# One inference step with 32 experts: expert weights loaded as pairs of chunks, and four buffers for the h2 rows

## What is computed

```python
h = x + mix
ff = _moe(_rmsnorm(h, norm2_g), router_w, router_b, w1, b1, w2, b2)
# in _moe, for each block of rows of one expert e:
a = xe @ w1[e] + b1[e]                      # w1[e] is 1024 x 2048
glu = jnp.minimum(a[:, 0::2], SWIGLU_LIMIT)
lin = jnp.clip(a[:, 1::2], -SWIGLU_LIMIT, SWIGLU_LIMIT)
act = glu * jax.nn.sigmoid(SWIGLU_ALPHA * glu) * (lin + 1.0)
yb = act @ w2[e] + b2[e]                    # w2[e] is 1024 x 1024
# y = sum over the 4 experts of a row of gate * yb; then h + y, and a last norm
```

## Time and profile before

| | |
|---|---|
| median of 3 runs | 1410.18 us (1409.35 to 1410.38) |
| the profiled execution's own time | 1410.55 us |
| its span, first to last instruction | 1408.6 us |
| mean granted clock of TensorE | 0.977 |
| PE busy | 1314.7 us, 93% |
| DVE, ACT, POOL busy | 336.8, 236.8, 313.1 us |
| moved by DMA | 476.19 MB, 338 GB/s over the span |

### The profile page before, as it was taken

How to read it: one execution, slowest core, us unless ns; L and a number is a source line. 1 busy time by engine, 2 the same in 40 slices (tenths; PEclk the granted TensorE clock), 3 DMA queues, 4 the chain that set the end, 5 groups by cost and what they waited for, 6 DMA issues and landing times.

```text
span 1408.6 us, 36025 instructions
## 1 busy us (share of the span) xinstructions
PE 1314.7 (93%) x15410; PEld 664.1 (47%) x15411; DVE 336.8 (24%) x570; ACT 236.8 (17%) x554; POOL 313.1 (22%) x321
## 2 busy tenths in 40 slices
PE   5999869987989999999999999999999999999993
PEld 5999547985333333333333333333333333434332
DVE  4322674246111121111111121111111111211111
ACT  5433674132000000010000000010000000000012
POOL 1200000102632222223322222223222222222212
PEclk9999799997999999999999999999999999999996
DMA  8523404775999999999999999999999999999996
GB/s 243 169 81 107 146 1 152 272 285 192 351 408 398 407 406 407 407 407 406 402 402 402 407 406 406 407 407 406 403 403 402 403 407 406 406 406 406 406 404 180
DMA packets 104039, 476.19 MB, mean 338 GB/s; under 512 B 14158, under 2 KB 39370, under 8 KB 54737
## 3 DMA queue, kind: packets, MB, share of 16 engines
q1 hardware_dynamic: 81769, 443.39, 78.5%
q0 software_dynamic: 22224, 32.16, 9.5%
HBM read 457.02 MB, written 22.34 MB: 340 GB/s over the span
## 4 chain that ended last, share of the span: by engine, by line
PE 65%; DMA 20%; SPq 6%; DVE 4%; issue 2%; ACT 2%; POOL 1%; POOLq 0%; DVEq 0%; ACTq 0%
PE ps L1794 31%; PE ps L1817 18%; DMA freed<-w 14%; PE ps L1512 10%; SPq L486 5%; DMA h_rows<-raw 1%; DMA arena<-h_rows,idx_t 1%; PE ps L1800 1%; PE ps L1638 1%; POOL slot_table L653 1%; PE ps L1688 1%; SPq L468 1%; DMA raw<-w_in 1%; DVE arena L1173 1%; DMA cst<-c_misc 0%
## 5 line engine op out<-in xcount | busy, mean ns | idle before, releaser
L1794 PE MATMUL ps<-freed,arena 128*32 128x512 f32 x2976 | 332.3, 595 | 13.2 <-DMA freed<-w 6.7
L1794 PE MATMUL ps<-raw,arena 128*32 128x512 f32 x2976 | 327.4, 593 | 2.6 <-DMA raw<-w 2.5
L1817 PE MATMUL ps<-freed,act_t 128*32 128x256 f32 x5952 | 326.7, 379 | 0.0
L1817 PEld LDWEIGHTS ps<-freed,act_t 128*32 128x32 f32 x5952 | 188.0, 110 | 133.6 <-issue 0.7
L645 POOL DMA_INDIRECT sum_rows<-arena,idx_s x87 | 137.7, 1582 | 487.9 <-issue 487.9
L1794 PEld LDWEIGHTS ps<-raw,arena 128*32 128x32 f32 x2976 | 92.3, 110 | 232.1 <-issue 211.1
L1794 PEld LDWEIGHTS ps<-freed,arena 128*32 128x32 f32 x2976 | 92.5, 110 | 231.2 <-issue 205.3
L1386 DVE TENSOR_SCALAR arena<-ps 128x512 f32<-128x512 f32 x64 | 32.7, 553 | 622.0 <-PE ps L1800 622.0
L983 ACT ACTIVATE arena<-ps 128x256 f32<-128x256 f32 x64 | 31.4, 491 | 672.3 <-PE ps L1800 663.6
L1512 PE MATMUL ps<-hi,t_hi 128*128 128x256 f32 x400 | 115.8, 290 | 3.1 <-ACT raw L807 1.7
L1512 PE MATMUL ps<-lo,t_hi 128*128 128x256 f32 x400 | 114.0, 285 | 0.0
(11 more groups left out here) (258 smaller groups left out, 881.4 us busy)
## 6 DMA issues: line engine op xcount, KB each, us to landing
freed<-w SPq DMA_DIRECT2D x256, 1024.0 KB, 24.0
raw<-w SPq DMA_DIRECT2D x128, 1024.0 KB, 22.8
raw<-w_in SPq DMA_DIRECT2D x8, 1024.0 KB, 6.6
raw<-cache_k SPq DMA_DIRECT2D x32, 256.0 KB, 4.6
raw<-cache_v SPq DMA_DIRECT2D x32, 256.0 KB, 5.1
raw<-w_out SPq DMA_DIRECT2D x4, 1024.0 KB, 4.9
raw<-x_prompt SPq DMA_DIRECT2D x4, 512.0 KB, 4.0
arena<-x_prompt POOLq DMA_DIRECT2D x4, 512.0 KB, 5.8
```

Source lines behind the costliest of these rows:

```text
L1794: last = pe.matmul(ps[TR * b:TR * b + TR, i, :], x_of[:, at:at + TR], w[:, 512 * b:512 * b + 512], start=j == 0, stop=False, tile_position ...
L1817: last = pe.matmul(ps[TR * b:TR * b + TR, 3 + i, 0:QD], act_of[:, at:at + TR], w[:, col:col + QD], start=g == 0 and half == 0, stop=g == W ...
```

## The change

Weights of experts are loaded two chunks at a time: one DMA of 2 MB, 16 KB contiguous per partition in memory and on the chip. Twelve single slots become six pair buffers (`pair_at`), each with one semaphore; PE waits at every even chunk. A pair buffer is free when both its chunks were multiplied. The semaphores of the projection weights are their own now (`s_pro`), and `split_hi` and `split_lo` name raw's slot directly. `h2` takes raw's third and fourth slots and has four buffers: only the fifth tile waits, for the first tile's transposes and its store (`s_h2a`), and POOL issues each store as soon as its rows are there. The last of the first six pairs waits for all stores.

```diff
+        def pair_at(q):
+            if q == 0:
+                return raw[:, 0:2, :]
+            if q == RAW // 2 - 1:
+                return raw[:, 2:4, :]
+            at = (0, 4, 2, 6)[q - 1]
+            return freed[:, at:at + 2, :]
+
         def raw_at(s):
-            if s < 3:
-                return raw[:, s, :]
-            if s < RAW - 1:
-                return freed[:, RING * ((s - 3) % 2) + (s - 3) // 2, :]
-            return raw[:, 3, :]
+            return pair_at(s // 2)[:, s % 2, :]
...
-        h2 = raw[:, 3, :].rearrange("p (a n) -> p a n", a=2)
+        h2 = raw[:, 2:4, :].rearrange("p s (a n) -> p (s a) n", a=2)
...
             def load_expert(ck, j, e, k, second_half):
 
+                q = ck.raw_slot(j) // 2
                 if second_half:
-                    src = a["w2"][0][bass.ds(e, 1)].rearrange("a (p k) n -> (a p) k n", k=KT)[:, 2 * k:2 * k + 2, :]
-                    dst = raw_at(ck.raw_slot(j)).rearrange("p (k n) -> p k n", k=2)
+                    src = a["w2"][0][bass.ds(e, 1)].rearrange("a (p k) n -> (a p) k n", k=KT)[:, 2 * k:2 * k + 4, :]
+                    dst = pair_at(q).rearrange("p s (k n) -> p (s k) n", k=2)
                 else:
-                    src = a["w1"][0][bass.ds(e, 1)].rearrange("a (p k) n -> (a p) k n", k=KT)[:, k, :]
-                    dst = raw_at(ck.raw_slot(j))
-                return sp.dma_start(dst, src).then_inc(s_raw[ck.raw_slot(j)], 16)
+                    src = a["w1"][0][bass.ds(e, 1)].rearrange("a (p k) n -> (a p) k n", k=KT)[:, k:k + 2, :]
+                    dst = pair_at(q)
+                return sp.dma_start(dst, src).then_inc(s_raw[q], 16)
 
             start = Chunks(PRO, 0)
-            for j in range(W1C):
+            for j in range(0, W1C, 2):
                 if j == 0:
                     sp.wait_ge(s_vd, 2)
-                if j >= 3:
-                    sp.wait_ge(s_w, len(OUT_UNITS) - RING + (j - 3) // 2 + 1)
+                if j >= 2:
+                    sp.wait_ge(s_w, len(OUT_UNITS) - (2 if j < 6 else 0))
                 load_expert(start, j, 0, j, False)
 
             def body_loads(n):
                 ck = Chunks(PRO + W1C, n)
-                for j in range(PER):
+                for j in range(0, PER, 2):
                     if not isinstance(n, int) or W1C + j >= RAW:
-                        sp.wait_ge(s_pc, ck.number(j) - PRO - RAW + 1)
-                    elif W1C + j == RAW - 1:
+                        sp.wait_ge(s_pc, ck.number(j) - PRO - RAW + 2)
+                    elif W1C + j >= RAW - 2:
                         sp.wait_ge(s_h2t, NT)
-                        sp.wait_ge(s_h2d, 16 * NT)
-                    else:
-                        sp.wait_ge(s_w, len(OUT_UNITS) - RING + (W1C + j - 3) // 2 + 1)
+                        sp.wait_ge(s_h2a, 16)
+                        sp.wait_ge(s_h2d, 16 * (NT - 1))
...
             for t, (r, n) in enumerate(TILES):
                 pool.wait_ge(s_h2, t + 1)
-                if t:
-                    pool.wait_ge(s_h2d, 16 * t)
-                pool.dma_start(h2_dram[r:r + n, :], h2[0:n, t % 2, :]).then_inc(s_h2d, 16)
+                pool.dma_start(h2_dram[r:r + n, :], h2[0:n, t % 4, :]).then_inc(s_h2d if t else s_h2a, 16)
...
-                if t >= 2:
-                    v.wait_ge(s_h2t, t - 1)
-                    v.wait_ge(s_h2d, 16 * (t - 1))
-                v.scalar_tensor_tensor(out=h2[0:n, t % 2, :], in0=h_res[0:n, SLOT_H[t], :], scalar=st[0:n, 36 + t:37 + t], in1=g2[0:n, :],
+                if t == 4:
+                    v.wait_ge(s_h2t, 1)
+                    v.wait_ge(s_h2a, 16)
+                v.scalar_tensor_tensor(out=h2[0:n, t % 4, :], in0=h_res[0:n, SLOT_H[t], :], scalar=st[0:n, 36 + t:37 + t], in1=g2[0:n, :],
...
-                pe.wait_ge(s_raw[ck.raw_slot(j)], ck.loaded(j))
+                if j % 2 == 0:
+                    pe.wait_ge(s_raw[ck.raw_slot(j) // 2], ck.loaded(j))
```

More of the change, by code:

```diff
@@ L296, in build @@
         s_late = sem("pool_inputs_loaded")
-        s_raw = [sem(f"raw_loaded{i}") for i in range(RAW)]
+        s_pro = {i: sem(f"projection_weights_loaded{i}") for i in (0, 2)}
+        s_raw = [sem(f"raw_pair_loaded{i}") for i in range(RAW // 2)]
         s_hi, s_lo = sem("hi_done"), sem("lo_done")
@@ L315, in build @@
         s_xr, s_w, s_he = [sem(f"x_reloaded{i}") for i in range(3)], sem("w_out_unit"), sem("h_unit")
+        s_h2a = sem("first_h2_stored")
         s_n2, s_r2, s_h2, s_h2d, s_h2t, s_h2e, s_lg, s_lge = (sem(n) for n in ("n2_squares", "n2_root", "h2_done", "h2_stored", "h2_transposed", "h2t_out", "router_done", "logits_out"))
@@ L382, in loaded @@
             def loaded(self, j):
-                before = {0: pro_loads(PRO - 1), 2: pro_loads(PRO - 2)}.get(self.raw_slot(j), 0)
-                return self.step * (16 * PER // RAW) + 16 * (before + (self.base + j - PRO) // RAW + 1)
+                return self.step * (16 * PER // RAW) + 16 * ((self.base + j - PRO) // RAW + 1)
         def further_blocks(eng, body):
@@ L418, in load_pro @@
                 src = w_in[:, :, 256 * g:256 * g + 256] if g < 8 else w_out[:, :, 256 * (g - 8):256 * (g - 8) + 256]
-                sp.dma_start(raw[:, pro_slot(g), :].rearrange("p (k n) -> p k n", k=KT), src).then_inc(s_raw[pro_slot(g)], 16)
+                sp.dma_start(raw[:, pro_slot(g), :].rearrange("p (k n) -> p k n", k=KT), src).then_inc(s_pro[pro_slot(g)], 16)
             load_x(0)
@@ L514, in _ @@
             tail = Chunks(PRO + W1C + PER * (NE - 1), 0)
-            for j in range(W2C):
-                sp.wait_ge(s_pc, tail.number(j) - PRO - RAW + 1)
+            for j in range(0, W2C, 2):
+                sp.wait_ge(s_pc, tail.number(j) - PRO - RAW + 2)
                 load_expert(tail, j, NE - 1, j, True)
@@ L615, in _ @@
                 pool.wait_ge(s_h2, t + 1)
-                if t:
-                    pool.wait_ge(s_h2d, 16 * t)
-                pool.dma_start(h2_dram[r:r + n, :], h2[0:n, t % 2, :]).then_inc(s_h2d, 16)
+                pool.dma_start(h2_dram[r:r + n, :], h2[0:n, t % 4, :]).then_inc(s_h2d if t else s_h2a, 16)
             pool.wait_ge(s_lge, NT)
             pool.wait_ge(s_tab, 3)
-            pool.wait_ge(s_h2d, 16 * NT)
+            pool.wait_ge(s_h2a, 16)
+            pool.wait_ge(s_h2d, 16 * (NT - 1))
             def alone():
@@ L729, in split_hi @@
             def split_hi(slot_raw, slot, loaded):
-                act_e.wait_ge(s_raw[slot_raw], loaded)
-                act_e.activation(hi[:, slot, :], raw_at(slot_raw), ACT.Copy).then_inc(s_hi, 1)
+                act_e.wait_ge(s_pro[slot_raw], loaded)
+                act_e.activation(hi[:, slot, :], raw[:, slot_raw, :], ACT.Copy).then_inc(s_hi, 1)
             def pro_hi(g):
@@ L1060, in split_lo @@
                 v.wait_ge(s_hi, hi_done)
-                v.tensor_tensor(lo[:, slot, :], raw_at(slot_raw), hi[:, slot, :].bitcast(F32), ALU.subtract).then_inc(s_lo, 1)
+                v.tensor_tensor(lo[:, slot, :], raw[:, slot_raw, :], hi[:, slot, :].bitcast(F32), ALU.subtract).then_inc(s_lo, 1)
             def pro_lo(g):
@@ L1714, in h2_transposes @@
                 for k in range(KT):
-                    last = pe.transpose(ps[:, k // 4, P * (k % 4):P * (k % 4) + n], h2[0:n, t % 2, P * k:P * k + P], ident[0:n, 0:n])
+                    last = pe.transpose(ps[:, k // 4, P * (k % 4):P * (k % 4) + n], h2[0:n, t % 4, P * k:P * k + P], ident[0:n, 0:n])
                 last.then_inc(s_h2t, 1)
```

## The result

The changed kernel takes **1432.2 us** (median of 5 runs, 1429.3 to 1434.4) against 1410.4 of the kernel before beside it: 1.0138 times as long, 95% interval 1.0111 to 1.0165. It is slower by 1.4%, outside the range given; the forecast was 1409.7. The profiled execution took 1434.4 us, with a span of 1432.5.

The account below looks back on a forecast made before the run. PE set the pace up to about 946 us, then weight loads did. Packets -8.6, slots +2.6 and the start of expert 2 +5.5 gave -0.5 us: 1409.7 us, own range 1401 to 1412, overall range 1397 to 1418.

Parts of the forecast that it names:

- In the rounds themselves the same turns cost nothing: Expert rounds: POOL's queue taking turns with 16 KB weight packets adds 0 us, as gathers land before DVE needs them.
- Some 5 us more, for twelve packets' turns, are within the 6.5 us that are left: Expert rounds: a gather's twelve packets take some 5 us longer, within 6.5 us left after DVE's 1.61 us.
- the sum: Whole kernel: -8.6 for packets, +2.6 for coarser slots, +5.5 before expert 2, together -0.5 us.
- Packets: Weight loads: 16 KB packets save 0.30 us an expert, 8.6 us over 28.7 experts; bounds nothing to 0.60 an expert.
- The rule weighed against it: Weight loads: a fixed 3 cycles or so per packet, so 0.17 us saved an expert and 1413.4 us in all.
- Router: Before the first w1: four h2 buffers end DVE's wait at tile 3, making the chain 5.0 us shorter, w1 at 340.0.
- POOL queue before expert 2: Stores and gather before expert 2: 0.78 us a turn, expert 2 starts at 413, no weights move from 410.9 to 419.9.
- Its price of 5.5 us: Before expert 2: the 33rd chunk starts at 419.9 instead of 414.4, 5.5 us more, with the router's 5.0 included.
- Coarser slots: End of the last w1: PE has two chunks left after the landing instead of one, 2.6 us more.
- Rivals: POOL turns unlengthened: 1400.7 us (0.23); half packet gain: 1414.0 (0.07), none: 1418.3 (0.12); still 8 KB packets: 1409.3 (0.08).
- wrong: in neither sum, DVE waiting for a gather in every round: Expert rounds: a listed sign that the forecast is wrong, with no size and no chance of its own.

## Why the prediction was wrong

The step that failed is this: **"In the rounds themselves the same turns cost nothing"**, with its reason, "Some 5 us more, for twelve packets' turns, are within the 6.5 us that are left". The mechanism (turns, packet by packet, 0.48 to 0.78 us) was in the text and was right; it was sized wrongly in two places.
- It counted twelve packets an engine. The scatter that POOL issues just before puts 24 of 1 KB more on the same queue, ahead of the gather's own. All 36 take 28.2 us with 16 KB, issues included, and in the run with two loads 18.8 (917.1, the first scatter's issue there, to 926.4 + 9.5): **9.4 us more**, not 5. (Twelve turns longer by 0.78 - 0.48 us would give 3.6, not 5; the prediction doesn't say where its 5 comes from.)
- It took the gather of the earlier trace rows as landed early, because DVE took the rows at 938.30 without a wait. With the 9.5 us of the run with two loads it landed at about 936.4, only 1.9 us ahead; the completions in the trace of the kernel before put it at 936.25 (in the run with two loads at 935.6). 9.4 - 1.9 = 7.5, and DVE's wait in the round shown is 7.54. The 6.5 us were PE's slack behind DVE: 7.54 - 6.5 leaves 1.0, and PE stalls 1.25 us at 909.22.

The small stall had a second price. PE's rounds came to 32.5 us (911.25 us for 28 rounds from 453.28), no faster than 16 KB loads that set the pace themselves (32.39). So PE never worked off the lead of loaded pairs, and what longer packets bring could not show: by the packets of the traces the last weights had landed 47.0 us before the end of the execution, in the run with the gather first 33.6.

Two of the 28 rounds lost more than the others. In each, POOL's second gather issue came some 15 us late, with no releaser in the trace, and that pair of rounds and the next were some 5 us longer than two other pairs. This is no accident of one run: the same two issues are late in every kernel with this order on POOL, and by the packet length again; with the gather first no issue there is more than 1.3 us late. The first of the two with 8 KB (the kernel before), with 16 KB (the changed one) and with 4 KB:

```profile
806.76 1.05 POOL L635 DMA_INDIRECT arena<-h_rows,idx_g  x1 [7.74 <-issue]
...
832.59 1.05 POOL L639 DMA_INDIRECT arena<-h_rows,idx_g  x1 [15.25 <-issue]
...
806.04 1.05 POOL L639 DMA_INDIRECT arena<-h_rows,idx_g  x1 [4.09 <-issue]
```

The run with the gather first takes the failed step away: 1411.8 against 1412.1 beside it, -0.4 us where the sum was -0.5. That agreement is luck: it rests on two terms that were off in opposite directions, below.

The other steps:
- **Packets.** 8.6 us from 0.30 us an expert; measured 0.41 (32.80 to 32.39), 11.8 us over 28.7 experts, and 13.7 us for the whole kernel with nothing else in the way. The kind was right, the size a quarter too small, inside its bounds. The rounds of 32.6 late in the stage came as 32.4 to 32.5 in the runs with gathers in time. From 4 to 8 KB the step is 33.68 - 32.80 = 0.88 us for 96 packets an engine less, from 8 to 16 KB 0.41 for 48: 9 ns a packet both times. The rule weighed against it, in the Trainium skill's "DMA: Bandwidth & Descriptors", section "Why small descriptors are slow (HBM only)", gave 0.17 us; the measurement decides, and it is over twice that.
- **Router.** Right for the norms, too much for what follows. The norms of the five tiles span 26.0 us (294.4 to 320.4), before 31.1 (291.8 to 322.9). But from the first norm to the first w1 it is 53.2 us before and 49.5 to 52.1 in the ten kernels with four buffers: 1.1 to 3.7 us come through, not 5.0. Behind the last norm PE does the same 307 matmuls at a lower granted clock, 0.52 on the average for 0.77. In the changed kernel it fell to the lower level, 0.50, after PE had been busy for 0.27 us of the 2 from 320 to 322, and stayed there until 346; before, it was at 0.88 again from 338 to 342. Before, and after (as the earlier trace rows):

```profile
323.00:345.00 22.00, 13.07 (x307) 10.37 (x308) 15.43 (x49) 4.50 (x12) 4.76 (x6) 0.77 0.50 172
...
320.50:345.90 25.40, 16.87 (x307) 12.92 (x308) 15.44 (x49) 4.62 (x12) 4.59 (x5) 0.52 0.69 289
```

  In three of the experiments the first w1 began at 339.92, 339.94 and 340.01, where 340.0 was forecast; that is luck, as their first norms began 2 to 3 us earlier (288.6, 289.2 and 289.7).
- **POOL queue before expert 2.** Right: 0.785 us a packet for 0.78, last landing after 29.3 us for 28. Expert 2 began at 419.30, 73.4 us after the first w1; forecast 413 after 340.0, 73. (The 410.9 us at which the loads were to run dry comes out at 410.1 from the prediction's own terms; it changes nothing.) The loads' rest is there too, but longer than the 9.0 us from 410.9 to 419.9: in the run with the gather first no packet of weights starts from 412.98 to 425.28, 12.3 us, and in the changed kernel from 416.35 to 428.01. The first pair comes free 8.7 to 9.2 us after expert 2's start, not 6.9, as the clock is at its lower level (0.50) when PE starts again:

```profile
411.00:420.00 9.00, 3.87 (x20) 1.02 (x24) 3.01 (x2) 0.00 (x0) 2.78 (x4) 0.50 0.17 59
413.00:425.00 12.00, 8.87 (x60) 2.42 (x64) 3.01 (x2) 0.00 (x0) 6.48 (x7) 0.65 0.17 30
```

- **Its price of 5.5 us** was too low. By the packets of the traces the 33rd chunk starts at 425.3 in the run with the gather first, for 415.1 before: 10.2 us, from the longer rest and from the router's gain that didn't come. Putting that gather ahead of the stores took 12 us out (1411.8 to 1399.6, same chip), which is the whole rest of 12.3 us; the prediction had 5.5 + 3.5 = 9.0 between the two.
- **Coarser slots.** 2.6 us. From the landing of the last weights to the end of the execution the traces have 30.8 to 31.1 us with single chunks (three kernels) and 32.5 to 34.1 with pairs (eight, without the changed kernel): 2.4 us on the average, so the term was about right.
- **Rivals.** None held; the likeliest way to lose had stood under "wrong: in neither sum, DVE waiting for a gather in every round", without a chance of its own. It deserved one, as the same mechanism was charged in full one paragraph earlier.

With these terms the sum for the run with the gather first is 10.2 + 2.4 - 11.8 = +0.8 us, against -0.4 by the medians and -2.0 to +3.2 by the interval. Open: why POOL's gather issue is late in just those two rounds.

## What to carry to other kernels

Longer packets on one queue sped that queue here and slowed the other queue on the same engines, for each turn holds one packet of the neighbour: count all packets ahead of the wanted one on its queue, not only its own. Before lengthening packets, order the small queue by due time (gathers ahead of scatters and stores) or put bulk stores in line with the weights; here that turned 1.4% lost into 0.7 to 1.0% gained. And "taken without a wait" doesn't say how early a transfer landed: look for a run or a row that shows the landing.

## What was not expected of the hardware

- A packet costs about 9 ns of an engine beside its bytes, the same from 4 to 8 KB as from 8 to 16 KB (0.88 us for 96 and 0.41 for 48), and one transfer of 2 MB with 8 KB packets is no faster than two of 1 MB (1.0015 and 1.0009).
- A gather landed 5.7, 9.5 or some 18 to 19 us after its issue by nothing but the packet length of another queue. From 4 to 8 KB the batch of scatter and gather grew less than the packets did (about 15 us to 18.8), since the issues alone take 9.3 us; from 8 to 16 KB it grew by half.
- 2.2 MB of stores took 30.7 us on POOL's queue beside weights in 16 KB packets, and 12.8 us in line with them.
